# Norms, last rows and feed-forward banks of a two-block transformer kernel, rearranged

## What is computed

```python
u = rms_norm(x, norm_g)                                       # n0
proj = u @ w_in                                               # 10 parts of 1024 columns
c = causal_depthwise_conv(cg * xc, conv_w)
y_conv = (silu(zc) * bg * c) @ w_out_conv
y_attn = (silu(za) * mixture_of_dilations(q, k, v)) @ w_out_attn
x = rms_norm(x + (sigmoid(g_conv) * y_conv + sigmoid(g_attn) * y_attn) @ w_o, final_g)   # n1
for layer in (0, 1):
    o_main = nsa_attention(...) if layer == 0 else moba_attention(...)
    o_mem = memory_attention(qm, mem, w_mem_kv)
    x = layer_norm(ALPHA * x + concat(o_main, o_mem) @ w_out, ln1)                       # n2, n4
    a, b = split(x @ ffn_w_in)
    x = layer_norm(ALPHA * x + (gelu(conv3(a) + conv_b) * b) @ ffn_w_out, ln2)           # n3, n5
```

## Time and profile before

| | us |
|---|---|
| median of three runs | 1001.85 (1001.05 to 1003.83) |
| the profiled execution | 1001.48 |
| its span | 999.7 |
| PE busy, 7006 matmuls | 948.9 (95%) |
| DVE busy | 664.5 (66%) |
| ACT busy | 527.0 (53%) |
| POOL busy | 127.9 (13%) |

### The profile page before, as it was taken

One profiled execution on the slowest core, in us unless ns is written; L12 is line 12 of the kernel. 1 busy time (PEld: TensorE's weight loads), 2 busy tenths in 40 slices (PEclk: granted clock), 3 DMA queues, 4 the chain that ended last, 5 costly groups with the idle time before them and its releaser, 6 DMA issues.

```text
span 999.7 us, 19995 instructions
## 1 busy us (share of the span) xinstructions
PE 948.9 (95%) x7006; PEld 859.3 (86%) x7006; DVE 664.5 (66%) x1212; ACT 527.0 (53%) x967; POOL 127.9 (13%) x154
## 2 busy tenths in 40 slices
PE   8999999999999888999799999998899989999995
PEld 5899999999899877757699999987788679999995
DVE  5566666666666857965866666678567666666666
ACT  5545555555444648754555555545565455555553
POOL 3000000000100402630600000006100150000001
PEclk9999999999999999999999999999999999999998
DMA  7555555556465375314265555553754346555552
GB/s 256 181 190 178 178 178 182 178 175 226 148 210 188 125 254 158 120 37 148 86 231 190 187 188 189 189 193 108 243 179 152 105 148 205 188 184 189 184 189 77
DMA packets 48226, 172.89 MB, mean 173 GB/s; under 512 B 6031, under 2 KB 6479, under 8 KB 48060
## 3 DMA queue, kind: packets, MB, share of 16 engines
q1 hardware_dynamic: 44732, 159.78, 47.9%
q0 software_dynamic: 3456, 12.61, 4.1%
HBM read 171.29 MB, written 1.07 MB: 172 GB/s over the span
## 4 chain that ended last, share of the span: by engine, by line
PE 77%; DVE 10%; ACT 6%; DMA 4%; issue 2%; POOL 1%; SPq 0%; POOLq 0%; ACTq 0%; DVEq 0%
PE bank L1330 17%; PE bank L1331 17%; PE bank L1332 17%; PE ysum L1378 6%; PE ysum L1380 6%; PE ysum L1379 6%; DVE sb_wl L815 5%; DMA sb_raw<-in_stream 4%; ACT sb_wh L417 2%; PE bank L1409 1%; PE ysum L1416 1%; PE ysum L1423 1%; ACT sb_xh L442 1%; DVE sb_z L861 1%; ACT sb_pr L462 1%
## 5 line engine op out<-in xcount | busy, mean ns | idle before, releaser
L815 DVE TENSOR_TENSOR sb_wl<-sb_raw,sb_wh 128x1024 fp32r<-128x1024 f32 x300 | 388.4, 1297 | 169.2 <-ACT sb_wh L417 168.3
L1330 PE MATMUL bank<-sb_xh,sb_wh 128*128 128x256 f32 x1360 | 383.3, 282 | 3.2 <-DVE sb_t_a L1242 2.5
L1331 PE MATMUL bank<-sb_xl,sb_wh 128*128 128x256 f32 x1360 | 379.8, 279 | 0.0
L1332 PE MATMUL bank<-sb_xh,sb_wl 128*128 128x256 f32 x1360 | 379.8, 279 | 0.0
L417 ACT ACTIVATE sb_wh<-sb_raw 128x1024 fp32r<-128x1024 f32 x300 | 315.0, 1055 | 116.2 <-PE ysum L1380 46.7
L1330 PEld LDWEIGHTS bank<-sb_xh,sb_wh 128*128 128x128 f32 x1360 | 256.3, 188 | 12.6 <-DVE sb_t_a L1242 3.5
L1332 PEld LDWEIGHTS bank<-sb_xh,sb_wl 128*128 128x128 f32 x1360 | 257.9, 190 | 0.0
L1331 PEld LDWEIGHTS bank<-sb_xl,sb_wh 128*128 128x128 f32 x1360 | 255.4, 188 | 1.5
L1378 PE MATMUL ysum<-sb_wh,sb_mh 128*128 128x512 f32 x208 | 81.7, 393 | 3.6 <-DVE sb_ml L825 3.6
L1379 PE MATMUL ysum<-sb_wl,sb_mh 128*128 128x512 f32 x208 | 81.7, 393 | 0.0
L1380 PE MATMUL ysum<-sb_wh,sb_ml 128*128 128x512 f32 x208 | 81.6, 393 | 0.0
(11 more groups left out here) (265 smaller groups left out, 1439.0 us busy)
## 6 DMA issues: line engine op xcount, KB each, us to landing
sb_raw<-in_stream SPq DMA_DIRECT2D x300, 512.0 KB, 3.3
sb_bias<-rel_rows POOLq DMA_DIRECT2D x12, 384.0 KB, 3.8
sb_bias<-in_alibi POOLq DMA_DIRECT2D x8, 256.0 KB, 3.1
sb_gb<-in_ln_g POOLq DMA_DIRECT2D x4, 512.0 KB, 4.1
sb_gb<-in_ln_b POOLq DMA_DIRECT2D x4, 512.0 KB, 6.5
sb_x_tok<-in_x SPq DMA_DIRECT2D x2, 512.0 KB, 3.9
sb_memf<-in_mem_t POOLq DMA_DIRECT2D x1, 1024.0 KB, 6.2
out<-sb_x_tok SPq DMA_DIRECT2D x2, 512.0 KB, 2.6
```

The lines of the kernel that those rows point to most:

```text
L815: dve.tensor_tensor(wl[slot][:, :, :], raw[slot][:, :, :], wh[slot][:, :, :].bitcast(F32), ALU.subtract).then_inc(split_l, 1)
L1330: pe.matmul(out, wh[slot][:, k, :], mov_h(k), start=k == 0, stop=False)
L1331: pe.matmul(out, wh[slot][:, k, :], mov_l(k), start=False, stop=False)
L1332: last = pe.matmul(out, wl[slot][:, k, :], mov_h(k), start=False, stop=k == KT - 1)
```

## The change

Nothing of what is computed changes, and no block is added or dropped.

- *Order of the parts.* In `stationary` and its kin the two matmuls with the high activations come first and the one with the low activations last. `two_stationary`, and the new `x_rows` for the value blocks of n0 and n3, do all high matmuls first and then the low ones.
- *Norms.* ACT makes all eight high parts from PSUM with the gain and shift applied, and `xf` 6 and 7 after them. DVE makes seven of the low parts, POOL only that of block 1. z is scaled in halves, and transposes start on a half. The transposes of tile 1 come in the middle of the second key or value block. `last_rows` orders the last two row blocks by token tile, so that `half` comes earlier.
- *Loops.* The stream is now: first, second, first, second, then row, first, second for each pair, with four banks for the products, so that the row of a pair comes a block pair later. The merge loop likewise.
- *Function tables.* `table_of` runs a tiny activation ahead of time, in front of the compressed keys and in n2, n3 and n4, so that its table is loaded there.
- *Gains.* `load_gb` goes behind the second pair of the scores, and into the middle of the feed-forwards and of the second attention; n3's tail now comes ahead of the biases with no load between.
- *Second attention.* The first pair's q and k blocks come ahead of the two wide value blocks.

```diff
+FETCHED = {nm: (0, 1, 2, 3, 4, 5) if nm in ("n0", "n3") else (4, 5, 0, 1, 2, 3)
+           for nm in ("n0", "n1", "n2", "n3", "n4")}
+LOW_DVE, LOW_POOL = (0, 2, 3, 4, 5, 6, 7), (1,)
...
-            bk = bank[(0 if nm in ("n0", "n3") else 4) + k // 2]
+            bk = bank[{"n0": (0, 1, 2, 3), "n3": (0, 1, 2, 4)}.get(nm, (4, 5, 6, 7))[k // 2]]
...
             def low_odd(nm):
 
-                for k in range(1, KT, 2):
+                for k in LOW_POOL:
+                    norm_wait(pool, nm, "xf", FETCHED[nm].index(k) + 1)
                     norm_wait(pool, nm, "xh", k + 1)
                     pool.tensor_tensor(xl[:, k, :], xf[:, k, :], xh[:, k, :].bitcast(F32), ALU.subtract
                                        ).then_inc(S[nm, "xl_pool"], 1)
...
             tail("n1", False)
-            norm_wait(pool, "n1", "x", 2)
-            load_gb(a["ln1_g_2"][0], a["ln1_b_2"][0])
             for i in range(PAIRS2):
                 if i + 1 < PAIRS2:
                     relative("p3", i + 1, 12)
+                if i == 1:
+                    norm_wait(pool, "n1", "x", 2)
+                    load_gb(a["ln1_g_2"][0], a["ln1_b_2"][0])
...
+            for nm, g, b, row, block in (("n2", "ln2_g_2", "ln2_b_2", 0, B_FFN0 + 18),
+                                         ("n3", "ln1_g_2", "ln1_b_2", 1, B_QK + 6),
+                                         ("n4", "ln2_g_2", "ln2_b_2", 1, B_FFN1 + 18)):
...
                 low_odd(nm)
                 tail(nm, True)
-                norm_wait(pool, nm, "x", 2)
-                load_gb(a[g][row], a[b][row])
                 if nm == "n3":
                     pool.wait_ge(S["p3", "max"], 12 * PAIRS2)
                     for i in range(PAIRS2):
                         relative("p5", i, 4)
+                norm_wait(pool, nm, "x", 2)
+                pool.wait_ge(used, block)
+                load_gb(a[g][row], a[b][row])
...
+            def table_of(function):
+
+                chain.link(act.activation(st[:, 12:13], half[:, :], function))
...
-                def high(k):
-                    if k < 6:
-                        norm_wait(act, nm, "xf", k + 1)
-                    else:
-                        norm_wait(act, nm, "xf_act", k - 5)
-                    act.activation(xh[:, k, :], xf[:, k, :], ACT.Copy).then_inc(S[nm, "xh"], 1)
-
-                for k in range(4):
-                    high(k)
-                norm_wait(act, nm, "turned", KT)
+                shift = [0.0 if b is None else gbt[:, b, k:k + 1] for k in range(KT)]
+                for k in range(KT):
+                    norm_wait(act, nm, "turned", k // 2 * 2 + 2)
+                    if k in (4, 5) and nm not in ("n0", "n3"):
+                        norm_wait(act, nm, "xf", 2)
+                    act.activation(xh[:, k, :], turned_x(nm, k), ACT.Identity, scale=gbt[:, g, k:k + 1],
+                                   bias=shift[k]).then_inc(S[nm, "xh"], 1)
                 for k in (6, 7):
-                    if k == 7:
-                        high(4)
-                    act.activation(xf[:, k, :], turned_x(nm, k), ACT.Identity,
-                                   scale=gbt[:, g, k:k + 1], bias=0.0 if b is None else gbt[:, b, k:k + 1]
-                                   ).then_inc(S[nm, "xf_act"], 1)
-                for k in range(5, KT):
-                    high(k)
+                    act.activation(xf[:, k, :], turned_x(nm, k), ACT.Identity, scale=gbt[:, g, k:k + 1],
+                                   bias=shift[k]).then_inc(S[nm, "xf_act"], 1)
...
+            table_of(ACT.Gelu_apprx_tanh)
             refill(0, b + 3)
...
             refill(0, B_KM)
+            table_of(ACT.Gelu_apprx_tanh)
             norm_high("n2", 2, 3)
             memory_keys(B_KM)
...
+                for i in range(2):
+                    b = b0 + 2 * i
+                    act.wait_ge(used, b + 1)
+                    base(i, i)
+                    refill(0, b)
+                    gelu(i)
+                    refill(0, b + 1)
+                    high(i, i)
+
+                def body(j):
+                    for c in range(2):
+                        b, i = b0 + 4 + 3 * c, j * 2 + (c + 2)
+                        refill(j, b, 6)
+                        act.wait_ge(used, j * 6 + (b + 2))
+                        base(i, c)
+                        refill(j, b + 1, 6)
+                        gelu(i)
+                        refill(j, b + 2, 6)
+                        high(i, c)
...
+            table_of(ACT.Exp)
             norm_high("n3", 4, 5)
...
                     pt_evac("p5", 2 * i - 1, pt[:, 0, 0, 0:CAUSAL], bank[5][:, 0:CAUSAL])
+                else:
+                    refill(0, b + 1)
+                    act.wait_ge(used, B_MOBA + 4)
+                    norm_wait(act, "n3", "x", 2)
+                    act.activation(v_all[:, 1, 0:512], bank[6][:, :], ACT.Copy).then_inc(v_up[1], 1)
+                    refill(0, B_VWIDE)
+                    refill(0, B_VWIDE + 1)
...
+            refill(0, B_FFN1 - 1)
+            table_of(ACT.Gelu_apprx_tanh)
             norm_high("n4", 6, 7)
-            refill(0, B_FFN1 - 1)
...
-                    norm_wait(dve, nm, "turned", k // 2 * 2 + 2)
+                    if nm in ("n0", "n3") or k < 4:
+                        norm_wait(dve, nm, "xh", k // 2 * 2 + 2)
+                    else:
+                        norm_wait(dve, nm, "turned", k // 2 * 2 + 2)
...
+                if nm in ("n0", "n3"):
+                    for k in FETCHED[nm]:
+                        fetch(k)
+                        if k in LOW_DVE:
+                            low_of(k)
+                        if k == 0 and between is not None:
+                            between()
+                else:
+                    for k in FETCHED[nm][:4]:
+                        fetch(k)
+                    low_of(0)
+                    for k in FETCHED[nm][4:]:
+                        fetch(k)
+                    for k in LOW_DVE[1:5]:
+                        low_of(k)
+                for k in (6, 7):
+                    low_of(k)
...
+                if soon is not None:
+                    refill(0, soon)
...
-                        norm_wait(dve, nm, "sum", t + 1)
-                        dve.tensor_scalar(z[:, t, :], z[:, t, :], st[:, 10 + t:11 + t], None,
-                                          ALU.mult).then_inc(S[nm, "z"], 1)
+                    norm_wait(dve, nm, "mean" if centred else "sum", t + 1)
+                    for n in range(2):
+                        part = z[:, t, n * 512:(n + 1) * 512]
+                        if centred:
+                            dve.tensor_scalar(part, part, st[:, 4 + t:5 + t], st[:, 10 + t:11 + t],
+                                              ALU.add, ALU.mult).then_inc(S[nm, "z"], 1)
+                        else:
...
+            with dve.Fori(0, KT // 2 - 1) as j:
+                for c in range(2):
+                    b, i = B_MIX + 4 + 3 * c, j * 2 + (c + 2)
+                    refill(j, b, 6)
+                    part_c(i, j * 6 + (b + 2), c)
+                    refill(j, b + 1, 6)
+                    part_a(i, j * 6 + (b + 3), c)
+                    refill(j, b + 2, 6)
...
+            def stationary(slot, out, mov_h, mov_l, k0=0, k1=KT):
+
+                for k in range(k0, k1):
+                    pe.matmul(out, wh[slot][:, k, :], mov_h(k), start=k == 0, stop=False)
+                    pe.matmul(out, wl[slot][:, k, :], mov_h(k), start=False, stop=False)
+                    last = pe.matmul(out, wh[slot][:, k, :], mov_l(k), start=False, stop=k == KT - 1)
+                if k1 == KT:
+                    last.then_inc(used, 1)
+
+            def two_stationary(b, nm):
+
+                ready(b + 2)
                 for k in range(KT):
-                    pe.matmul(out, wh[slot][:, k, :], mov_h(k), start=k == 0, stop=False)
-                    pe.matmul(out, wh[slot][:, k, :], mov_l(k), start=False, stop=False)
-                    last = pe.matmul(out, wl[slot][:, k, :], mov_h(k), start=False, stop=k == KT - 1)
-                last.then_inc(used, 1)
...
+                    norm_wait(pe, nm, "xh", k + 1)
+                    for n in range(2):
+                        out, s = bank[n][:, 0:T], slot_of(b + n)
+                        pe.matmul(out, wh[s][:, k, :], xh[:, k, :], start=k == 0, stop=False)
+                        pe.matmul(out, wl[s][:, k, :], xh[:, k, :], start=False, stop=False)
                 for k in range(KT):
...
+                        last = pe.matmul(bank[n][:, 0:T], wh[slot_of(b + n)][:, k, :], xl[:, k, :],
+                                         start=False, stop=k == KT - 1)
                         if k == KT - 1:
                             last.then_inc(used, 1)
...
+            def x_rows(nm, slot, parts, out, n_first=False):
+
+                def part(w, j, n):
+                    j = n if n_first else j
```

(103 more changed lines are left out.)

339 lines of the change are left out of this document (115 added, 224 removed).

## The result

1011.45 us (median of five, 1009.18 to 1013.33) against 1001.85: ratio 1.0085, 95% interval 1.0071 to 1.0100. The change is slower, by 8.5 us at the ratio, 9.6 by the medians.

What follows compares the result with a forecast made beforehand. PE bounds the long loops, so only time between them, around the norms, can change. Terms 0.2 + 0.1 + 0.1 - 2.7 - 0.7 + 0.3 + 2.5 + 3.0 + 0.5 + 4.0 - 0.25 = +7.0; 1001.5 + 7.0 = 1008.5, range 1001 to 1015.

Steps and rivals of the forecast that it cites:

- rival 1: Behind the norms, DVE's low parts take turns with POOL's tail: 1008.5, range 1001 to 1015; chance 0.50.
- The deciding step: At the norms, DVE's low parts wait on POOL's tail (x gain + shift); third norm: PE waits 7.9 on value block three.
- the turns: DVE's low parts and POOL's 1024-column steps exclude each other, one instruction each; low parts 2.6 apart beside the tail.
- The clock: PE falls to 1.2 GHz behind its waits at the second, third and fourth norm: 2.3 each, 0 as lower end.
- Gain loads: Moving `load_gb` from the compression stage's start: -2.7 (0 to -4.0); its new place in the scores: +0.3 (0 to 1.2).
- Merge stage: Merge loop: later rows hide ACT's copies of the memory, -0.8, and the last row costs 0.9: +0.1.
- The last row's 0.9: End of merge stage and first feed-forward: PE waits 0.9 for the last row's low part.
- Start: Norm at the start: high matmuls begin 0.9 sooner, but weight block 2 waits behind seven low parts: +0.2.
- First pair of the second attention: Values around first q and k: last values' copy and a weight low part precede the first minimum on DVE: +0.5.
- Rival 2: At the norms, low parts slip through, as the tail starts later or DVE keeps the port: 985; chance 0.30.
- give-back: In rival 2, the tail falls on weight low parts behind: about 10 (2.1 behind the first norm, then 3, 3, 2).
- Rival 3: At the norms, the waits of rival 1 occur but the clock holds: 1001.6, no change that can be told; chance 0.17.

Runs made afterwards that it cites:

- the tail later: Changed kernel, POOL's tail (steps of 1024 columns) starting in every norm only after DVE's seven low parts: 0.9903, 994.0 us.
- the old division: Changed kernel with low parts divided as before, DVE the even ones, POOL the odd ones ahead of its tail: 0.9884, 992.7 us.
- the new one alone in the other kernel: Kernel before, only the low parts redivided: DVE makes seven, POOL that of block 1 alone: 1.0125, 1016.8 us.
- short steps: Changed kernel with POOL's tail cut into steps of 256 columns instead of 1024: 0.9877, 989.8 us.
- seven low parts with the tail moved off: Changed kernel, POOL's tail moved into the feed-forward loops, behind the fourth projection (first norm) and behind DVE's seven (third): 0.9827.
- filled kernel: Changed kernel with matmuls on zeros where PE waits, at the second, third and fourth norm: 1.0007, 1003.7 us.
- the tail in the loops: POOL's tail spread over feed-forward pairs, behind the fourth projection at the first norm; with old division 0.9824, 985.6 us; in the kernel before 0.9960, 997.6 us.

## Why the prediction was right, and what was off in it

The forecast was 1008.5, for rival 1 at 0.50; the time is 3 above, inside its own range of 1001 to 1015. It rests on the step that the runs bear out, not on luck, though two smaller terms, of the start and of the compression stage, were off by 1 and 2. By stage, from the starts on PE's timeline, each as the difference of the two profiled executions:

| stage | forecast | profile |
|---|---|---|
| start and head pairs | +0.2 | +2.3 |
| merge | +0.1 | +0.8 |
| first norm, compression | -3.3 | +0.95 |
| scores, rows | +0.7 | +1.1 |
| second norm, four blocks | +2.1 | +1.9 |
| first feed-forward loop | +0.9 | +0.8 |
| third norm to first scores | +2.1 | +1.5 |
| second attention, rows | +0.9 | +0.1 |
| fourth norm, four blocks | +3.6 | +3.5 |
| to the end | -0.25 | -1.0 |
| sum | +7.05 | +11.9 |

The last column is that of one execution, the slowest of five. With the start and the compression stage at their means over the profiles (+1.1 and -1.6, below) it sums to +8.2, near the 8.5 of the ratio.

**The deciding step held**, in place and in size. Third norm: transposes at E+3.35 and E+5.7 (3.5 and 5.9 were given), the tail at E+9.6 (10.2), the held low parts 2.5 to 2.6 apart (2.6), low part 7 done at E+20.3 (20.8), the wait on the third value block 7.88 (7.9). Second norm: tail at E+10.1 (10.35), low 7 at E+20.9 (21.2). First norm: the weights behind the two blocks at E+17.2 (17.6). That the turns are the cause is shown from five sides: the tail later, the old division, the new one alone in the other kernel, short steps, and seven low parts with the tail moved off. As to the page that I named, the Trainium skill, SBUF — State Buffer, section "SBUF: two separate sides", with its lock held for a whole instruction: the short steps agree (a low part of weights beside steps of 256 columns 1.7, beside steps of 1024 columns up to 3.4), and who goes next is, in the stretches shown here, the other side each time, of which the section says nothing.

**The clock held**: 2.3 a norm was given, 2.4, 2.35 and 2.1 are measured between two profiles, and 7.8 for the run as a whole. It makes almost all the difference between the change and no change.

**What failed.** (1) *Gain loads*, -2.7 + 0.3: alone the move measures -1.5 (0 to -2.9). The compression stage does get 2.3 shorter; my 0.3 for the place where the load now stands was too small, 1.4 in that profile, which the clock covers that fell there (0.10 x 17 = 1.7). It does not fall in each execution: of eleven profiles with the moved load five, the changed kernel's among them, have 1.00 in that stretch (396 to 412) and six 0.79 to 0.89; the three with the load in its old place have 1.00. (2) *Merge stage*: "Rows one pair later hide ACT's copies of the memory, -0.8" is wrong. The wait of 0.82 on a weight low part moved from a stationary block to the row behind it and stayed. The last row's 0.9 was right (0.87). (3) *Start*: with rebuilt norms the merge begins at 258.4 to 260.7, mean 259.4 over ten profiles, with the old norms at 257.9 to 258.9; so about +1.1 instead of +0.2. In the profile of the change it is 2.3, where the first weight block was taken up at 9.2 instead of 7.8 and the clock fell to 0.93. (4) *First pair of the second attention*, +0.5: nothing was to be seen.

**The +0.95 of the compression stage is mostly the execution.** The filled kernel runs the same program up to the second norm and took 54.1 from E to the compressed keys, the changed kernel 57.4; over the ten kernels with rebuilt norms it is 53.1 to 57.4, mean 54.6, over the two with old norms and the load in its old place and the old division, 55.9 and 56.5. So the step was worth about -1.6 for my -3.3. About half of the 3.3 between the filled and the changed kernel's profiles is clock: from 340 to 360, behind the waits of the first norm, the mean is 0.83 in the changed kernel and 0.91 in the filled one and in the kernel before (0.08 x 20 = 1.6). What made up the rest I can't tell.

**The rivals.** Rival 2 (low parts slip through, 985) did not happen. The late tail is the kernel that it describes, with low parts 0.4 apart and the tail on the weight low parts behind; it took 994.0, so rival 2 was priced 9 too low. The gain over the changed kernel was 18 by the ratios, not 1008.5 - 985 = 23.5. Part of that is a give-back put too small: from E of the second norm to the fourth block it took 25.3 with the late tail and 19.6 with seven low parts and the tail in the loops, 5.7 for my 3; at the fourth norm 21.2 and 18.2, 3.0 for my 2. That 984.1 and 985.6, with the tail in the loops, lie at rival 2's number is chance: for these its sum without the give-back would have been 975. Rival 3 is the kernel with PE kept busy, 1003.7, 2 above what it gave.

## What to carry to other kernels

When DVE and POOL both work on two SBUF inputs and both have work queued, the price was here one POOL instruction for each DVE instruction; so count the instructions that DVE still owes at the moment POOL starts, not POOL's busy time. Taking work off POOL may bring its next, longer work forward into DVE's critical row: look at what its queue holds next, and put long steps where DVE owes nothing urgent, or cut them short. Waits of 2 us one behind the other, or one of 8, can cost PE again behind them in clock, here 2.1 to 2.4 at each of three norms.

## What the hardware showed that I had not expected

The turns, wherever both queues were full in the stretches above, are strict in both directions and per instruction. Beside steps of 256 columns a low part of a tile that was held up took about 0.95, beside steps of 1024 columns 2.0 to 2.6.

The clock's fall is not the same in each execution of one program. In the first 26 us it was 1.00 in the kernel before and 0.93 in the one that differs from it only later (the tail in the loops); 0.93 in the changed kernel and 1.00 in the filled one, also the same up to there. At the second pair of the scores (396 to 412) it was 1.00 with the tail in the loops and 0.89 in the kernel that differs from that one only at the start. That may be part of the 4 us by which executions of one kernel differ here.
